# Head norms of queries and keys by token and head instead of by channel, in the first two layers of a three-layer kernel

## The reference

```python
def rms_norm(x, g):
    xf = x.astype(jnp.float32)
    y = xf * lax.rsqrt(jnp.mean(xf * xf, axis=-1, keepdims=True) + EPS)
    return (y * g.astype(jnp.float32)).astype(x.dtype)
...
        if i % 2 == 0:
            q = rms_norm(q.reshape(B, S, FOX_HEADS, HEAD_DIM), fox_g_q[j])
            k = rms_norm(k.reshape(B, S, FOX_HEADS, HEAD_DIM), fox_g_k[j])
...
    q = rms_norm(xq.reshape(B, S, MEM_HEADS, HEAD_DIM), g_q)
    k = rms_norm(mk.reshape(B, M, MEM_HEADS, HEAD_DIM), g_k)
```

## Time and profile before

| | us |
|---|---|
| median of three runs | 1848.2 (1847.42 to 1849.12) |
| profiled execution | 1850.17 |
| its span | 1848.3 |
| TensorE busy in the span | 1803.7 (98%) |
| VectorE | 1436.0 (78%) |
| ScalarE | 1150.3 (62%) |
| GpSimd | 200.7 (11%) |

### The profile page before, as it was taken

The page is one execution under the profiler, slowest core; times in us unless marked ns, Lnnn a source line. Parts: engine busy times, 40 slices in busy tenths (PEclk is TensorE's granted clock), DMA queues, the critical chain, the costliest instruction groups (busy, mean ns, idle before and its releaser), DMA issues.

```text
span 1848.3 us, 27953 instructions
## 1 busy us (share of the span) xinstructions
PE 1803.7 (98%) x10792; PEld 1595.2 (86%) x10792; DVE 1436.0 (78%) x1332; ACT 1150.3 (62%) x1130; POOL 200.7 (11%) x157
## 2 busy tenths in 40 slices
PE   8988999999999999999999999999999999899998
PEld 7977999999878888888888888888887899799998
DVE  6855877779768888988888888888889867665553
ACT  5545434356767777777777777777777757543332
POOL 0032111121020000000000000000007002302221
PEclk9999999999999999999999999999999999999998
DMA  9603688842259999999999999999999943235530
GB/s 393 262 21 149 240 335 326 318 176 88 78 221 386 373 377 390 363 388 380 373 383 368 403 372 370 398 365 386 382 365 422 373 178 137 92 115 183 183 138 23
DMA packets 74574, 520.88 MB, mean 282 GB/s; under 512 B 8064, under 2 KB 8192, under 8 KB 13952
## 3 DMA queue, kind: packets, MB, share of 16 engines
q1 hardware_dynamic: 73056, 514.02, 72.7%
q0 software_dynamic: 1440, 5.77, 0.8%
HBM read 504.02 MB, written 15.73 MB: 281 GB/s over the span
## 4 chain that ended last, share of the span: by engine, by line
PE 93%; DVE 4%; ACT 1%; issue 1%; DMA 0%; POOL 0%; DVEq 0%; SPq 0%; ACTq 0%
PE ps L1253 28%; PE ps L1255 27%; PE ps L1254 27%; PE ps L1500 1%; PE ps L1662 1%; PE ps L1283 1%; DVE wl L1875 1%; PE ps L1430 1%; PE ps L1451 1%; PE ps L1276 1%; PE ps L1267 0%; DVE sqz L1868 0%; DVE nmx L2045 0%; DVE big L1868 0%; PE ps L1309 0%
## 5 line engine op out<-in xcount | busy, mean ns | idle before, releaser
L1875 DVE TENSOR_TENSOR wl<-raw,wh 128x2048 fp32r<-128x2048 f32 x446 | 1027.0, 2305 | 256.2 <-ACT wh L773 143.2
L1079 ACT ACTIVATE wh<-raw 128x2048 fp32r<-128x2048 f32 x336 | 644.9, 1920 | 181.8 <-PE ps L1255 181.2
L1253 PE MATMUL ps<-wh,xh 128*128 128x512 f32 (+1 forms) x1040 | 396.4, 381 | 1.4 <-DVE wl L1875 1.4
L1255 PE MATMUL ps<-wh,xl 128*128 128x512 f32 (+1 forms) x1040 | 390.0, 375 | 0.0
L1254 PE MATMUL ps<-wl,xh 128*128 128x512 f32 (+1 forms) x1040 | 389.6, 375 | 0.0
L1253 PE MATMUL ps<-xh,wh 128*128 128x256 f32 x1152 | 331.8, 288 | 8.0 <-DVE xl L1875 5.6
L1254 PE MATMUL ps<-xl,wh 128*128 128x256 f32 x1152 | 327.0, 284 | 0.0
L1255 PE MATMUL ps<-xh,wl 128*128 128x256 f32 x1152 | 326.8, 284 | 0.0
L773 ACT ACTIVATE wh<-raw 128x2048 fp32r<-128x2048 f32 x107 | 204.4, 1911 | 175.6 <-PE ps L1255 171.9
L1253 PEld LDWEIGHTS ps<-xh,wh 128*128 128x128 f32 x1152 | 222.1, 193 | 13.1 <-issue 9.8
L1253 PEld LDWEIGHTS ps<-wh,xh 128*128 128x128 f32 x1040 | 195.9, 188 | 36.8 <-DVE wl L1875 2.6
(11 more groups left out here) (304 smaller groups left out, 1952.0 us busy)
## 6 DMA issues: line engine op xcount, KB each, us to landing
raw<-in_experts SPq DMA_DIRECT2D x336, 1024.0 KB, 6.9
raw<-in_units SPq DMA_DIRECT2D x134, 1024.0 KB, 6.0
x_rows<-big SPq DMA_DIRECT2D x1, 6144.0 KB, 36.0
big<-x_rows SPq DMA_DIRECT2D x8, 512.0 KB, 7.8
y_rows<-big SPq DMA_DIRECT2D x7, 512.0 KB, 8.4
y_rows<-big SPq DMA_DIRECT2D x1, 2560.0 KB, 41.7
big<-in_mem SPq DMA_DIRECT2D x1, 1024.0 KB, 6.9
hT<-in_x SPq DMA_DIRECT2D x1, 1024.0 KB, 8.9
```

The lines of the kernel that those rows point to most:

```text
L1079: act.activation(wh[:, p % SPL, :], raw[:, n % RAW, :], ACT.Copy).then_inc(sem("hi_ready"), 1)
L1253: mm(out_, lh, rh, start=start, stop=False, **kw)
L1255: return mm(out_, ll, rh, start=False, stop=stop, **kw)
L1875: return V.tensor_tensor(out_, whole, leading.bitcast(F32), ALU.subtract)
```

## The change

The sums are now formed by token: the squares are the stationary operand (four blocks of 128 channels by 128 tokens), and two columns of `headones` move past them, so that a bank holds 128 tokens by 8 numbers (4 heads by 2 groups of tokens). Root and reciprocal act on these eight columns. VectorE then copies each number 64 times (`rq_by_head`, 128x512), TensorE transposes the four blocks back to channels (`head_spread`, into a new session `qrms` of the same bank), and ScalarE copies that bank to SBUF over `rq_by_head` (`qk_spread`). The scaling reads it there. In the first layer the spread of unit k = j stands half-way through the unit `UNITS_A[3 + j]` on TensorE, and its scaling moves to the head of VectorE's iteration j, ahead of that iteration's split. In the second layer spread 8 stands behind mq1 and spread 9 behind ci3; the scalings of mk1 and mq1 each move behind one more split.

```diff
@@ ScalarE
                 if k >= 2:
-                    wait_drained(act, QK_UNITS[k - 2])
-                act.activation(att_p[:, k % 2, :], bank(f"qsum{k}"), ACT.Sqrt, scale=1.0 / HD,
+                    wait_filled(act, f"qrms{k - 2}")
+                act.activation(rq[:, k % 2, :], bank(f"qsum{k}")[:, 0:8], ACT.Sqrt, scale=1.0 / HD,
                                bias=eps).then_inc(drained(f"qsum{k}"), 1)
+
+            def qk_spread(k):
+
+                wait_filled(act, f"qrms{k}")
+                act.activation(flat(rq_by_head), bank(f"qrms{k}"), ACT.Copy).then_inc(drained(f"qrms{k}"), 1)
...
                 name = UNITS_A[3 + j]
                 qk_square(2 + j, name)
+                qk_spread(j)
                 split_after(name)
                 qk_sd(1 + j)
...
                 values_out(f"fv{j}", vv[:, :, T * j:T * j + T])
+                if j < 2:
+                    qk_spread(6 + j)
                 if j == 0:
                     qk_sd(7)
...
             qk_square(9, "mq1")
+            qk_spread(8)
             split_after("mq1")
...
                 if n == 0:
                     qk_sd(9)
+                elif n == 1:
+                    qk_spread(9)
@@ TensorE
-                mm(bank(f"qsum{k}"), headones, att_pT[:, k % 2, :], start=True, stop=True).then_inc(filled(f"qsum{k}"), 1)
+                for a in range(2):
+                    for t in range(TT):
+                        at = 4 * a + 2 * t
+                        ins = mm(bank(f"qsum{k}")[:, at:at + 2], att_pT[:, k % 2, T * a + P * t:T * a + P * t + P],
+                                 headones[:, 0:P:HD], start=True, stop=True, skip_group_check=True)
+                ins.then_inc(filled(f"qsum{k}"), 1)
+
+            def head_spread(k):
+
+                pe.wait_ge(sem("qk_rms"), k + 1)
+                claim(pe, f"qrms{k}")
+                for a in range(2):
+                    for t in range(TT):
+                        at, to = 4 * a + 2 * t, T * a + P * t
+                        ins = pe.transpose(bank(f"qrms{k}")[:, to:to + P],
+                                           rq_by_head[:, at:at + 2, :].rearrange("p a b -> p (a b)"), ident)
+                ins.then_inc(filled(f"qrms{k}"), 1)
...
             for j in range(6):
-                by_channels(UNITS_A[3 + j])
+                by_channels(UNITS_A[3 + j], half_done=lambda: head_spread(j))
                 head_sum(1 + j)
...
-            by_tokens("fv0")
+            by_tokens("fv0", half_done=lambda: head_spread(6))
             head_sum(7)
-            by_tokens("fv1")
+            by_tokens("fv1", half_done=lambda: head_spread(7))
...
             by_channels("mq1", ready=arriving("mix1"))
+            head_spread(8)
             for name in CI_ORDER:
                 by_channels(name)
                 if name == "ci0":
                     head_sum(9)
+                elif name == "ci3":
+                    head_spread(9)
@@ VectorE
+            def head_root(k):
+
+                wait_drained(dve, f"qsum{k}")
+                link(V.reciprocal(rq[:, k % 2, :], rq[:, k % 2, :]))
+                V.tensor_copy(rq_by_head[:, :, :],
+                              rq[:, k % 2, :].unsqueeze(2).broadcast_to([P, 8, HD])).then_inc(sem("qk_rms"), 1)
...
-                r = att_p[:, k % 2, :]
-                wait_drained(dve, f"qsum{k}")
-                link(V.reciprocal(r, r))
+                wait_drained(dve, f"qrms{k}")
...
-            dve.wait_ge(sem("keys_zeroed"), 1)
-            keys("mk0", kz, FOX_HEADS, col(V_GMK))
+            head_root(0)
...
             for j in range(6):
+                if j == 0:
+                    dve.wait_ge(sem("keys_zeroed"), 1)
+                    keys("mk0", kz, FOX_HEADS, col(V_GMK))
+                elif j == 1:
+                    qk_scale("mq0", [(qT[:, 6:8, :], 0, P, gq8[:, 1:2])])
+                elif j < 5:
+                    qk_scale(f"fq{j - 2}", [(qT[:, 2 * j - 4:2 * j - 2, :], 0, P, gq8[:, 0:1])])
+                else:
+                    dve.wait_ge(sem("rows_zeroed"), 32)
+                    keys("fk0", kz, 0, col(V_FGK))
                 split_after(UNITS_A[3 + j])
+                head_root(1 + j)
...
+            keys("fk1", kz, 4, col(V_FGK))
+            head_root(7)
             keys("fk2", kz, 8, col(V_FGK))
...
             split_after("mv1")
+            head_root(8)
+            split_after("mq1")
             dve.wait_ge(sem("keys1_zeroed"), 1)
             keys("mk1", mkz1, 0, col(V_GMK + 1))
-            split_after("mq1")
...
             split_after("ci0")
-            qk_scale("mq1", [(q1[:, :, :], 0, P, gq8[:, 2:3])])
+            head_root(9)
             gated(0)
             split_after("ci3")
+            qk_scale("mq1", [(q1[:, :, :], 0, P, gq8[:, 2:3])])
             dve.wait_ge(sem("glu"), 1)
```

More of the change, by code:

```diff
@@ L269, in build @@
         rcol = sb("rcol", [P, TT])
+        rq = sb("rq", [P, 2, 8])
+        rq_by_head = sb("rq_by_head", [P, 8, HD])
         sub_c = sb("sub_c", [P, 4, TT])
@@ L365, in build @@
         S.add("qsum0", 4)
+        S.add("qrms0", 4)
         S.add("foxf", 2)
@@ L370, in build @@
         S.add("qsum1", 5)
+        S.add("qrms1", 5)
         S.add("cum", 6)
@@ L374, in build @@
             S.add(f"qsum{1 + j}", 4 + (1 + j) % 2)
+            S.add(f"qrms{1 + j}", 4 + (1 + j) % 2)
         product("fv0", 7)
         S.add("qsum7", 5)
+        S.add("qrms7", 5)
         product("fv1", 6)
@@ L434, in build @@
         S.add("qsum8", 0)
+        S.add("qrms8", 0)
         product("mq1", 3)
@@ L439, in build @@
                 S.add("qsum9", 4)
+                S.add("qrms9", 4)
         for j, c in enumerate(PE_CHUNKS):
@@ L1946, in norm_shifted @@
                             ALU.subtract).then_inc(sem("norm_lo_dve"), 1)
+            def head_root(k):
[3 more added lines that the diff above has]
+                              rq[:, k % 2, :].unsqueeze(2).broadcast_to([P, 8, HD])).then_inc(sem("qk_rms"), 1)
             def qk_scale(name, outs):
                 k = QK_UNITS.index(name)
-                r = att_p[:, k % 2, :]
-                wait_drained(dve, f"qsum{k}")
-                link(V.reciprocal(r, r))
+                wait_drained(dve, f"qrms{k}")
                 heads = bank(name).rearrange("p (a b) -> p a b", a=2)
-                r2 = r.rearrange("p (a b) -> p a b", a=2)
+                r2 = flat(rq_by_head).rearrange("p (a b) -> p a b", a=2)
                 for dst, lo, hi, gain in outs:
@@ L1997, in _ @@
             for j in range(6):
+                if j == 0:
[8 more added lines that the diff above has]
+                    keys("fk0", kz, 0, col(V_FGK))
                 split_after(UNITS_A[3 + j])
+                head_root(1 + j)
                 if j == 0:
-                    qk_scale("mq0", [(qT[:, 6:8, :], 0, P, gq8[:, 1:2])])
                     wait_lo(dve, "x")
```

## The result

The changed kernel took 1874.1 us (median of four runs, 1873.25 to 1875.2) against 1848.2: a ratio of 1.0137, interval 1.0122 to 1.0152. That is 25.9 us slower. The forecast was 1870.7 and its range 1862 to 1879.

A forecast was written before the change was run, and what follows sets the result against it. TensorE was taken as the bound, busy 98% of the span. First layer 15.3, second layer 3.8 and two clock falls of 1.7 each made 22.5 us on 1848.2: 1870.7 us, range 1862 to 1879.

The forecast's parts named there:

- The wait in the middle of a unit: First layer, fq1 to fv0: TensorE stands 1.99 us half-way, units 9.25 us for 6.61; layer sum 15.3 us.
- The step through both queues: From a unit's end at 65.56 through ScalarE's square, copy, split and VectorE's split, root, copy: TensorE goes on at 71.39.
- The sum and the spread: TensorE's added work: head sum 0.96 us for 0.86, spread 0.44 when ready; ten of both 5.4 us.
- The second layer: Spread 8 before ci0 waits behind two splits: ci0 3.26 us later, gap 4.43 for 1.71; layer sum 3.8 us.
- The clock: Granted clock falls to 0.50 behind the 4.43 us gap and one of five 1.99 us gaps: 1.7 us each.
- the rival of five falls: Clock falls behind all five first-layer gaps: four more falls, 6.8 us, total 1877.5 us; chance 0.17.
- The reading that transposes keep the clock: Transposes count as work for the clock gate, since the clock came back at about 188 us after mostly transposes.
- What is saved hides: VectorE's ten reciprocals (3.35 us) and ScalarE's ten roots shrink, but TensorE waits for neither: 0 us.
- The scalings behind ScalarE's copy: VectorE's scalings wait for ScalarE's copy but end before the next split would start: 0 us; uncovered, a key scaling adds 1.5.
- The rival of dearer transposes: Ten spreads run at 0.229 us a transpose, adding 4.7 us: 1875.4 us; chance 0.03.
- the rival of spreads in time: Roots reach TensorE before the unit's middle, leaving only 5.4 us: 1853.6 us; chance 0.06.
- the faster and the unchanged case: Faster: VectorE's queue is the bound, 1826.6 us, chance 0.02. Unchanged: partial cover of both kinds, chance 0.02.

The follow-up runs named there:

- moving the spreads: Changed kernel with the first layer's seven spreads behind their units instead of half-way through: 1857.2 us, ratio 1.0049.
- the version without waits: Changed kernel with the first layer's spreads behind their units and spread 8 behind ci0: 1853.7 us (1.0025), run again 1853.1 us (1.0033).
- the second profile with these gaps: Profile of the changed kernel with only spread 8 moved behind ci0, first layer as in the changed kernel: 1870.1 us, ratio 1.0109.
- the version with the first move alone: Changed kernel with only the first layer's seven spreads moved behind their units, spread 8 left before ci0: 1857.2 us, ratio 1.0049.
- The filled gaps: Changed kernel with 114 added transposes of a constant on TensorE ahead of its waits for VectorE's copy: 1867.6 us, ratio 1.0106.
- the first version with two passes: Kernel before the change with full-precision head sums in two fp32r passes, GpSimd subtracting, mq0's square not yet moved: 1850.1 us, ratio 1.0011.

## Why the prediction was right

**The wait in the middle of a unit** is the mechanism, in the six units named, and it was shown by moving the spreads: 17 us of 25.9. The cycle was put at 9.25 us and is 9.40. The step through both queues was right to 0.1 us (the reciprocal starts 5.12 us after the square's start at 59.80, 5.13 by the working); the copy ends and hands over 0.49 after its start for 0.47, and four transposes behind a gap take 0.66, not 0.54. In five units the term is 13.95 for 13.2. ScalarE reads out the last values at 124.22 us, for 104.39 before: 19.8 us later, which the 15.3 of the working and three falls (4.6) add up to.

**The sum and the spread.** A sum was put at +0.10 us. Its eight passes take 0.79, 0.07 less than before, but with the start-up behind them it is +0.04. The spread is 0.44 as taken. Ten of both were put at 5.4 and are 4.8 by the chain; the version without waits is 4.6 to 6 above the kernel before.

**The second layer.** The gap before ci0 was put at 4.43 and is 4.49, and no other wait came with it: TensorE's waits from 390 to 480 us have nothing else over 0.3.

**The clock** is the term that was mis-sized. One fall of five was taken for the first layer, and the trace has three (four in the second profile with these gaps). In the second layer one fall of 1.7 us was taken and two in a row came, 3.4 (behind the same gap one in the version with the first move alone, two in the version with the square behind its split). Had both been right, 1.7 + 1.7 would have been 4.6 + 3.4, and the forecast 1875.3. The bounds (0 to 8.5 in the first layer) held it, and the rival of five falls at 1877.5 was as near as the forecast. The filled gaps show the term by itself. How many falls a run draws was not something the rows could give, and the miss of 3.4 us has the size of two of them; one fall more or less, and with it a nearer or farther forecast, would have been luck. The reading that transposes keep the clock from a stretch "made mostly of transposes" up to 188 us was thin: they fill about 1.9 of the 3.4 us at half clock there. The filled gaps carry that point instead.

**What is saved hides** was right: 27.6 us of VectorE's work are gone, and the version without waits has gained nothing by it. The scalings behind ScalarE's copy cost nothing, as forecast.

The rival of dearer transposes fell with the version that issues each three times, the rival of spreads in time with the first trace, and the faster and the unchanged case with the time itself.

## What to carry to other kernels

When work moves from an engine with time to spare to the one that sets the end, count first what that engine pays (here 0.5 us a unit), and then place the consumer by the latest producer: follow the producer's queue from the event that starts it, and compare with where the in-order engine will stand. Here the middle of a unit was 2 us too early and its end was in time, with no wait. The cheaper lever was on the busy engine itself: fewer passes for the same sum, with the extra work given to engines with time to spare, once the producer came in time.

## What the runs showed of the hardware

- Gaps of 2.1 us in an otherwise dense TensorE queue let the clock fall to 0.50 behind three of five in one execution and four of five in another; gaps of 1.3 us on average, 1.5 at most, did not in the one execution profiled. Behind a gap of 4.5 us the half clock lasted 6.8 us in two executions and 3.4 in a third.
- Transposes in the gap kept the clock at 1.00 behind the five gaps of 2.1 us and the one of 4.5, in the execution profiled. The Trainium skill ("TensorE: Matmul & The Clock Gate", Part 4: PE-mode transpose) says that they don't count as work for the gate; with gaps of 2.1 and 4.5 us filled by float32 transposes to 0.6, the granted clock of 1.00 speaks against it, and the measurement decides.
- Where the clock falls differs from one execution to the next of the same kernel (37.4 and 18.1 us at half clock in two of them, with spans of 1850.8 and 1844.4 us). A difference of 2 or 3 us between two kernels needs many runs.
- A subtraction of 128x512 on GpSimd took 1.3 us in most units, 2.4 in one and 3.4 in another of the first version with two passes, for 2.77 on average in the feed-forward networks of the kernel before (line 683 on its page).
